# Three attentions woven one step deeper: scores of head h, turning of h-1 and applying of h-2 in one slot, and other tiles ahead of the second block's first head

## What is computed

```python
def first_block(x, ...):                       # one layer
    glu_in, q, k, v, gate_logits = split(rms_norm(x) @ w_in)
    a = silu(rms_norm(causal_conv(a_val * sigmoid(a_gate))));  y_a = a @ w_conv_out
    # per head: scores q k^T with three dilations, softmax mixed over them, times v
    y_b = dilated_attention(rms_norm(q), rms_norm(k), v) @ w_attn_out
    x = x + (g_a * y_a + g_b * y_b) @ w_out
    return x + ffn(rms_norm(x))

def dsa_mixer(x, ...):                         # layer a
    q, k, v, g, qi, wi, ki = split(x @ w_in)   # q, k, qi, ki get rotary embeddings
    score = sum over 8 index heads of relu(qi ki^T) * wi
    idx = top_k(score, 128)                    # per query; others are masked
    p = softmax(q k^T at idx, else -inf)
    return ((p @ v) * silu(g)) @ w_out

def stick_breaking_mixer(x, ...):              # layer b
    q, k, v, g = split(x @ w_in);  z = q k^T * scale
    a = exp(log_sigmoid(z) + reverse cumulative sum of log_sigmoid(-z) over later keys)
    return ((a @ v) * silu(g)) @ w_out
```

## Time and profile before

| what | value |
|---|---|
| median of 3 runs | 1728.77 us (1726.53 to 1730.64) |
| the profiled execution | 1727.02 us |
| its span, first to last instruction | 1725.2 us |
| PE busy | 1541.8 us, 89% |
| DVE busy | 1136.6 us, 66% |
| ACT busy | 745.3 us, 43% |
| POOL busy | 345.1 us, 20% |
| mean granted TensorE clock | 0.951 |

### The profile page before, as it was taken

One profiled execution on the slowest core, in us unless ns is written; L12 is line 12 of the kernel. 1 busy time (PEld: TensorE's weight loads), 2 busy tenths in 40 slices (PEclk: granted clock), 3 DMA queues, 4 the chain that ended last, 5 costly groups with the idle time before them and its releaser, 6 DMA issues.

```text
span 1725.2 us, 19424 instructions
## 1 busy us (share of the span) xinstructions
PE 1541.8 (89%) x6990; PEld 1267.2 (73%) x6990; DVE 1136.6 (66%) x2108; ACT 745.3 (43%) x1464; POOL 345.1 (20%) x277
## 2 busy tenths in 40 slices
PE   8889997879999999999999998588966979999878
PEld 7667886767878788888887777466755867777666
DVE  6735688888855477367365579667754464777766
ACT  6464643555353344244244341345534224555541
POOL 3622355213411111211211110100000111100101
PEclk9998998999999999999999999789987999999989
DMA  5444424532333233323323433554432336534413
GB/s 204 129 109 110 116 75 123 137 96 70 91 131 96 80 115 98 99 89 98 107 78 114 142 89 86 140 129 111 115 86 68 122 105 158 135 103 122 122 42 129
DMA packets 74048, 188.56 MB, mean 109 GB/s; under 512 B 10720, under 2 KB 16224, under 8 KB 73696
## 3 DMA queue, kind: packets, MB, share of 16 engines
q1 hardware_dynamic: 73952, 187.33, 38.2%
HBM read 137.48 MB, written 6.29 MB: 83 GB/s over the span
## 4 chain that ended last, share of the span: by engine, by line
PE 58%; DVE 26%; ACT 8%; issue 3%; DMA 2%; SPq 2%; POOL 0%; DVEq 0%; ACTq 0%
PE bank L588 13%; PE bank L589 13%; PE bank L590 13%; PE bank L601 4%; PE bank L603 4%; PE bank L602 4%; DVE ptl L1129 3%; DVE bank L1193 3%; DVE wlo L1119 2%; ACT p L1012 2%; DVE p L1182 1%; DVE mtab L1553 1%; DVE p L1553 1%; PE bank L628 1%; SPq L1672 1%
## 5 line engine op out<-in xcount | busy, mean ns | idle before, releaser
L1596 POOL TENSOR_TENSOR wlo<-raw,whi 128x512 fp32r<-128x512 f32 x225 | 305.3, 1363 | 1306.6 <-ACT whi L831 1306.5
L588 PE MATMUL bank<-xh,whi 128*128 128x512 f32 x1000 | 407.3, 407 | 11.1 <-DVE sgb L1484 7.6
L589 PE MATMUL bank<-xl,whi 128*128 128x512 f32 x1000 | 401.5, 402 | 0.0
L590 PE MATMUL bank<-xh,wlo 128*128 128x512 f32 x1000 | 400.4, 400 | 0.0
L831 ACT ACTIVATE whi<-raw 128x512 fp32r<-128x512 f32 x466 | 282.8, 621 | 254.6 <-PE bank L590 148.7
L588 PEld LDWEIGHTS bank<-xh,whi 128*128 128x128 f32 x1000 | 196.3, 196 | 52.3 <-DVE sgb L1484 8.1
L590 PEld LDWEIGHTS bank<-xh,wlo 128*128 128x128 f32 x1000 | 195.0, 195 | 43.6
L589 PEld LDWEIGHTS bank<-xl,whi 128*128 128x128 f32 x1000 | 195.9, 196 | 40.2 <-issue 0.5
L1119 DVE TENSOR_TENSOR wlo<-raw,whi 128x512 fp32r<-128x512 f32 (+1 forms) x241 | 177.2, 745 | 65.6 <-ACT whi L831 48.3
L1193 DVE SCALAR_TENSOR_TENSOR bank<-cbuf,vec,bank 128x512 f32<-128x512 f32 x240 | 164.4, 746 | 13.8 <-PE bank L590 7.6
L601 PE MATMUL bank<-whi,xh 128*128 128x512 f32 x340 | 136.5, 402 | 9.5 <-DVE xl L1129 7.3
(11 more groups left out here) (239 smaller groups left out, 2596.3 us busy)
## 6 DMA issues: line engine op xcount, KB each, us to landing
raw<-wst SPq DMA_DIRECT2D x224, 512.0 KB, 3.7
stack<-tmpr SPq DMA_DIRECT2D x152, 128.0 KB, 2.4
stack<-fresh SPq DMA_DIRECT2D x64, 128.0 KB, 2.4
stack<-turnr SPq DMA_DIRECT2D x40, 128.0 KB, 2.4
u<-bias SPq DMA_DIRECT2D x16, 256.0 KB, 2.8
rows<-scratch SPq DMA_DIRECT2D x8, 512.0 KB, 6.8
raw<-wst SPq DMA_DIRECT2D x8, 384.0 KB, 3.1
xr<-xt SPq DMA_DIRECT2D x8, 256.5 KB, 6.5
```

The lines of the kernel that those rows point to most:

```text
L588: e.matmul(bank[:, :], h[:, c], a, start=g + i == 0, stop=False)
L589: e.matmul(bank[:, :], h[:, c], b, start=False, stop=False)
L590: m = e.matmul(bank[:, :], l[:, c], a, start=False, stop=g + i == nk - 1)
L1596: e.tensor_tensor(wlo[k % NHL][:, 0:n], raw[u % NRAW][:, c:c + n], whi[k % NHL][:, 0:n].bitcast(F32), ALU.subtract).then_inc(*WLP.tick(k))
```

## The change

Slots. `weave_heads` now writes S of head h, the first half of the slot's projection halves, A of head h-2, T of head h-1, and the rest. All three units of scores, and all three of turning, stand together. An attention therefore has two more slots behind its last head instead of one.

Tiles. In layer a the values and the first tiles are put in the order of `FRONT`: 16 halves of query, key and gate tiles stand ahead of head 0's scores (12 before), the first query tile in the middle of the values. Queries and keys follow with two halves in each of slots 0 to 11, the last four gate tiles from slot 11 on.

Banks. Scores and turnings of the second block share one ring of four banks (2 to 5); the tiles ahead of head 0 use the same four.

Times within the plan. Rotations stand at least 2.5 us of planned work behind their tile, and not at a T or A step; ACT's split and SP's stacking one step later, DVE's low part two steps later. Closing a pair is spread over three steps likewise. Normalising is one step later where a projection half follows. SP's requests for weights stand four steps behind the freeing step in the first block's heads. POOL makes all the low weight parts from `va1` to the slot of head 0 (`selecting`), where before it made one in three.

```diff
+FRONT = lambda va1, tiles: (va1[:4] + tiles("q", 0) + va1[4:] + tiles("k", 0) + tiles("g", 0) + tiles("q", 1) + tiles("g", 1)
+                            + tiles("k", 1) + tiles("g", 2) + tiles("g", 3))
+G_SLOT = [0] * 11 + [1] + [2, 2, 2, 1]
+QK_SLOT = [2] * 12 + [0] * 4
+TURN_US = 2.5
+LOAD_LATER = {"": 4, "a": 1, "b": 1}
+TURN_NOT = "TA"
+SCORE_BANKS = {"": ((2, 3, 4), (2, 3, 4)), "a": ((2, 3, 4, 5), (2, 3, 4, 5)), "b": ((2, 3, 4, 5), (2, 3, 4, 5))}
...
-def weave_heads(h, chunks, prep=(), x=""):
...
-    if x == "" and h > 8:
-        return S + c[0] + T + list(prep[:1]) + c[1][:1] + list(prep[1:]) + c[1][1:] + A + c[2]
-    return T[:2] + S[:1] + c[0] + T[2:] + S[1:] + list(prep[:1]) + c[1][:1] + list(prep[1:]) + c[1][1:] + A + c[2]
+def weave_heads(h, chunks, prep=(), x="", heads=range(16)):
+
+    n = len(chunks) // 2
+    c, d = list(chunks[:n]), list(chunks[n:])
+    S = [("S" + x, h, u) for u in range(3) if h in heads]
+    T = [("T" + x, h - 1, u) for u in range(3) if h - 1 in heads]
+    A = [("A" + x, h - 2) for _ in range(1) if h - 2 in heads]
+    return S + c + A + T + list(prep[:1]) + d[:1] + list(prep[1:]) + d[1:]
...
-    T = [("T", 7, u) for u in range(3)]
-    p += T[:2] + q1[:2] + T[2:] + q1[2:4] + [("A", 7)] + q1[4:] + k1
+    rest = weave_heads(8, q1[:4], heads=range(8)) + weave_heads(9, q1[4:], heads=range(8))
+    p += rest + k1
...
-    size = [2] * 6 + [1, 1, 4]
-    for h in range(8, 17):
+    size = [2] * 6 + [1, 1, 2, 2]
+    for h in range(8, 18):
...
-            p += tiles("qkg", 0) + tiles("qkg", 1)
-            c = [half for n in range(2, 6) for half in tiles("qkg", n)]
-            c += tiles("qk", 6) + tiles("qk", 7) + tiles("g", 6) + tiles("g", 7)
-            size = [3, 2] * 4 + [3, 2] + [2, 2, 2, 2] + [2, 1]
+            front = FRONT(va1, tiles)
+            p += front
...
-        tail = weave_heads(16, [], x=x)
-        p += tail[:2] + o0[:4] + tail[2:3] + o0[4:8] + tail[3:] + o0[8:]
+        p += weave_heads(16, o0[:8], x=x) + weave_heads(17, o0[8:16], x=x) + o0[16:]
...
+TURN_HIGH_AT = {i + 1: n for i, n in TURN_AT.items()}
+TURN_LOW_AT = {i + 2: n for i, n in TURN_AT.items()}
...
+            at[i + 1 + (PLAN[i + 1][0] in FEAT)] = x[:2]
...
-    on_pool = lambda k: k in alone or k % 3 == 2
+    selecting = range(W.of["va1",][0], W.of[PLAN[PLAN.index(("Sa", 0, 2)) + 1][:2]][0])
+    on_pool = lambda k: k in alone or k in selecting or k % 3 == 2
```

More of the change, by code:

```diff
@@ L162, in make_plan @@
         if x == "a":
-            p += tiles("qkg", 0) + tiles("qkg", 1)
-            c = [half for n in range(2, 6) for half in tiles("qkg", n)]
-            c += tiles("qk", 6) + tiles("qk", 7) + tiles("g", 6) + tiles("g", 7)
-            size = [3, 2] * 4 + [3, 2] + [2, 2, 2, 2] + [2, 1]
+            front = FRONT(va1, tiles)
+            p += front
+            qk = [half for n in range(2, 8) for half in tiles("qk", n) if half not in front]
+            g = [half for n in range(8) for half in tiles("g", n) if half not in front]
+            c, size = [], []
+            for h in range(16):
+                n, m = G_SLOT[h], QK_SLOT[h]
+                c += qk[:m] + g[:n]
+                size.append(len(g[:n] + qk[:m]))
+                g, qk = g[n:], qk[m:]
         else:
@@ L254, in banks_in_order @@
     bank, n, heads, late = {}, 0, 0, False
-    rings = {"first": (0, 1, 2, 3, 4, 5, 6, 7), "pair": (0, 1), "six": (0, 1, 2, 3, 4, 6), "three": (0, 1, 7), "late": (0, 1, 7, 2, 3, 4, 5, 6),
+    rings = {"first": (0, 1, 2, 3, 4, 5, 6, 7), "pair": (0, 1), "six": (0, 1, 2, 3, 4, 6), "front": (2, 3, 4, 5), "tiles_a": TILE_BANKS["a"], "tiles_b": TILE_BANKS["b"], "late": (0, 1, 7, 2, 3, 4, 5, 6),
              "values": (0, 1, 6, 7)}
@@ L271, in banks_in_order @@
                 "late" if x[:2] in (("bq", 0), ("bk", 0)) else
-                "three" if name in ("aq", "ak", "ag", "bq", "bk", "bg") else
+                "front" if name in ("aq", "ak", "ag") and ("Sa", 0, 0) not in bank else
+                "tiles_" + name[0] if name in ("aq", "ak", "ag", "bq", "bk", "bg") else
                 "values" if name in ("va0", "va1") else
@@ L337, in turn_plan, with normal_plan, load_plan @@
 def turn_plan():
-    steps = [i for i, x in enumerate(PLAN) if x[0] in ("aq", "ak", "ag")]
+    us = lambda x: 2.7 if x[0] in FEAT or x[0] in TOK else 0.4 if x[0][0] in "ST" else 1.1
     at = {}
-    for n, i in enumerate(steps):
-        x = PLAN[i]
-        if x[0] != "ag" and x[2] == 1:
-            at[steps[n + 1]] = 2 * x[1] + (x[0] == "ak")
+    for i, x in enumerate(PLAN):
+        if x[0] in ("aq", "ak") and x[2] == 1:
+            j, t = i + 1, 0.0
+            while t < TURN_US or PLAN[j][0][0] in TURN_NOT:
+                t += us(PLAN[j])
+                j += 1
+            at[j] = 2 * x[1] + (x[0] == "ak")
     return at
 TURN_AT = turn_plan()
+TURN_HIGH_AT = {i + 1: n for i, n in TURN_AT.items()}
+TURN_LOW_AT = {i + 2: n for i, n in TURN_AT.items()}
+def normal_plan():
+    at = {}
+    for i, x in enumerate(PLAN):
+        if x[0] in ("S", "Sa") and x[2] == 2:
+            at[i + 1 + (PLAN[i + 1][0] in FEAT)] = x[:2]
+    return at
+NORMAL_AT = normal_plan()
+def load_plan():
+    at, last, later = {}, 0, 1
+    for i, x in enumerate(PLAN):
+        if x[0] in ("S", "Sa", "Sb"):
+            later = LOAD_LATER[x[0][1:]]
+        elif x[0] not in FEAT and x[0][0] not in "STAP":
+            later = 1
+        last = max(last, i + later)
+        at.setdefault(last, []).extend(k + NHL for k in W.freed.get(i, ()) if k + NHL < W.n)
+    return at
+LOAD_AT = load_plan()
 def close_plan(x):
```

74 lines of the change are left out of this document (36 added, 38 removed).

## The result

| | before | changed |
|---|---|---|
| time, median | 1727.65 us (1722.56 to 1730.64, 4 runs) | 1642.22 us (1639.73 to 1643.59, 4 runs) |
| ratio | | 0.9507, 95% interval 0.9481 to 0.9533 |
| span of the profiled execution | 1725.2 us | 1637.9 us |
| granted clock, mean | 0.951 | 0.968 |

What follows compares the result with a forecast made beforehand. PE was taken to carry the kernel, waiting mostly for DVE and ACT, with DVE next in layer a's slots. Savings of 11 + 7 + 68 + 25 = 111 from 1727.0 us gave 1616, range 1582 to 1678.

Steps and rivals of the forecast that it cites:

- Sign and stages: Whole kernel: faster, chance 0.91; savings of 11 in heads 0 to 7, 7 in heads 8 to 15, 68 in a, 25 in b.
- no rival as written: Loop keeps its length (1671 us, 0.18); PE alone (1583, 0.11); clock stays down (1754, 0.06); as before (1727, 0.03).
- A slot of layer a, 11.4: Layer a slots with a rotation: DVE's work of 10.2 us plus 1.2 of waiting, between 9.3 and 13.8.
- Slots 12 to 14 of layer a, 28.5: Layer a, three slots taken to have no rotations: 9.5 us each, 28.5 together.
- The end of layer a, 34: Layer a, last head with first o-projection: 25.4 us of halves, 7.1 of scores, applyings and turnings, 1.5 of waits.
- The front, 80: Layer a ahead of head 0: first score step 80 us behind the values (bounds 76 to 88), in place of 85.5.
- The port: Layer a's front: POOL pieces block DVE's two-input steps; by the rule 4 us more, 1620 in place of the sum.
- Heads 8 to 15, 7: First block, heads 8 to 15: 103.7 us in place of 110.8, saving 7 (bounds -3 to 14).
- Heads 0 to 7, 11: First block, heads 0 to 7: waits for the tanh vanish, saving 11 us (bounds 5 to 15).
- Layer b, 25: Layer b: slots of 12.25 us in place of 13.67, thirteen saving 18.5, three at the end 8; saved 25 (6 to 40).
- The ring of four: Rival that shared banks tie each turning to the score step before it, leaving slots as they were: 1727 us, chance 0.03.
- a clock under 0.75: Rival: PE's waits in each slot hold it at half clock, slots of 17.4 us, total time 1754 us; chance 0.06.

## Why the prediction was right or wrong, step by step

- **Sign and stages: right.** The largest part is layer a, the next b, and no rival as written came: slots in a are 11.6, neither 14 nor 9.3, and the clock in layer a rose to 0.94. The gain was forecast 111 and is 85 (87 between the profiled executions). Of the 24 missing there, layer a has 14.4 (slots 12 to 14 6.7, its end 4.2, the rest spread), heads 0 to 7 4.7, layer b 4.4, and the stretch behind heads 8 to 15, put at nothing, 3.6; heads 8 to 15 gave 3.6 more than forecast.
- **A slot of layer a, 11.4: right in size (11.6), half wrong in reason.** PE is not the bound and DVE's loop is; undoing the depth in a brought slots of 13.2 and 50.0 us of turnings waiting for normalising. But the term was built as DVE's 10.2 of work plus 1.2 of waits. DVE was busy 85.7 of 104.3 us from head 2 to 11, 9.5 a slot, and idle 2.1. Taking work away left the slot (8.9 busy, 11.8 in all), and changing the order alone shortened it. It is the way through DVE, ACT and DVE again, in the order as written, that lasts.
- **Slots 12 to 14 of layer a, 28.5: wrong, 35.2.** The step said these have no rotations. A rotation stands 2.5 us of planned work and more behind its tile, so the last query and the last key are rotated as slot 12 begins and in it, at 1221.57 and 1226.02; PE then waits 3.79 us for the split, and slot 13 takes 15.3 us. In the run with the gates moved the query's rotation starts earlier, 9.6 us ahead of slot 12, and slot 13 takes 13.0; that run moved a gate half too, so the rotations are not the only difference.
- **The end of layer a, 34: 38.2; and of b.** A wait of 4.7 and one of 6.6 at the o-projections, put down as 1.5 each. With the gates moved layer a waits 5.12 there, and b 2.81 with 2.2 ahead of a score; the ends hardly got shorter. The last heads have no halves left to hide DVE behind.
- **The front, 80: wrong, 85.0, made up by heads 0 and 1.** The chain is right link by link; the top-k's end was put at 57 and came at 61, and DVE had 2 us more to do and wait for at the last link. The two errors, 5 too early and 3.5 too long, nearly cancel in head 2's scores (95 and 96.5): that is luck. Moving the first query's rotation into the top-k, for which the prediction changed the order of tiles, did not bring the step forward: with the old order of 12 halves it comes at 78.9.
- **The port: the row was right to be weighed, its price was not seen in the sum.** The row put three DVE pieces beside one of POOL at 2.96 us; a run showed a rotation step at 1.63 in place of 0.68. The pieces on POOL brought that step 10.5 us forward; with POOL in the slots too, layer a lost 5. The Trainium skill, "SBUF — State Buffer", section "SBUF: two separate sides", has the loser blocked for the whole of the other's instruction; the step of 1.63 began 0.22 behind a POOL piece of 1.30 and ended 0.55 behind its end, and agrees. The cost that the prediction estimated from it, 4 us for eight steps met, did not come: of 21 DVE steps of 128x512 with both inputs in SBUF between the values and the first score step, one took longer than 0.9 us (1.45).
- **Heads 8 to 15, 7: 10.6, or 9.0 with the stretch behind them, in part for another reason.** The prediction put the gain on what PE has to do while 12 DMAs run, and took the later requests for weights for a risk. Its three pairs of heads came as it said (67.8 for 66.9, one of the waits for stacks 2.95 in place of 1.7 to 1.9); heads 14, 15 and the two draining slots took 32.5 in place of 36.8. But with the requests at once the same order takes 111.8, and its waits for stacks grow by 8.1: in the new order the price of 9.6 for the 12 DMAs holds only with the later requests. Depth counts too (107.7 without it): neither gives the gain alone.
- **Heads 0 to 7, 11: 6.3.** The tanh is hidden as said. The first small transpose's low part costs 4.8 us in three waits, put at 1.5, and the drain into the next projection takes 2.7 longer than before, put at 2.
- **Layer b, 25: 20.6, slots of 12.25 right (12.29 from head 2 to 12).** The saving a slot was too high: up to head 12 the slots before were 13.5 on average, not 13.67, and there are twelve of them, so they gave 14.6 in place of 18.5. The three behind gave 10.9 in place of 8, and the end was 4.9 longer, put at 1.5.
- **The ring of four: missed.** It was named only as a way in which the change might give nothing. Without it the change would have been slower than before by 3.05%, with slots of 16.0 in layer a at a granted clock of 0.88. That was the mechanism on the other side; the prediction had looked for it in a clock under 0.75.

## What to carry to other kernels

A deeper pipeline between in-order engines needs its buffers with it: count, for every group of steps that now stand together, the banks that they hold until the other engine has them. In such a loop look for the last engine's waits and what stands ahead of them, not for its sum of work: an instruction that needs nothing new should fill the wait, and a result that others wait for should not stand behind one that waits longer. At a pipeline's two ends the moved work piles up, so cost the ends one by one.

## What the runs showed of the hardware

Small DMAs behind a large one on one queue landed late: 128 KB in 2.3 us with no load just ahead, 4.1 to 4.8 us when 512 KB were issued 0.4 us ahead, at the same place and from the same engine. A DVE step with two SBUF operands took 0.68 us alone and 1.63 us beside a POOL subtraction of 1.30.
